# Turning finished attention results in three batches per head pair instead of tile by tile, in a two-layer streaming encoder on one Trainium2 core

## What is computed

```python
# layer 0: latent attention of 8 heads, then the shared output projection
s = (q_lat . ckv + q_rope . krope) * MLA_SCALE
p = softmax(where(visible, s, -inf));  o_lat = p @ ckv
x = x + concat([ha, hb], -1) @ w_out          # hb: o_lat through w_uv
# layer 1: band attention, 16 heads, a frame sees its chunk and the 8 before it
s = (q . k) * C_SCALE + rel_bias[:, idx]
p = softmax(where(valid, s, -inf));    o = p @ v
x = x + o.reshape(..., C_WIDTH) @ w_out_c
```

## Time and profile before

| | |
|---|---|
| median of 3 runs | 3217.87 us |
| lowest, highest | 3217.01, 3220.33 us |
| the profiled execution's own time | 3225.16 us |
| its span, first to last instruction | 3223.4 us |
| mean granted TensorE clock | 0.978 of 2.4 GHz |
| mix0b, its attention loop | about 504 to 799 us |
| mix1, its attention loop | about 1702 to 2364 us |

### The profile page before, as it was taken

How to read it: one execution, slowest core, us unless ns; L and a number is a source line. 1 busy time by engine, 2 the same in 40 slices (tenths; PEclk the granted TensorE clock), 3 DMA queues, 4 the chain that set the end, 5 groups by cost and what they waited for, 6 DMA issues and landing times. The chain is left out here.

```text
span 3223.4 us, 46994 instructions
## 1 busy us (share of the span) xinstructions
PE 3048.7 (95%) x18992; PEld 2941.0 (91%) x18992; DVE 1134.7 (35%) x2568; ACT 976.0 (30%) x1665; POOL 853.0 (26%) x436
## 2 busy tenths in 40 slices
PE   6999997999899999999989999999989999999998
PEld 5889896888799999999979999999869999999997
DVE  4423245566322222222243444444552222222223
ACT  4322234443412121111134444444442111211211
POOL 3212112110423222222242323223233222232320
PEclk8999998999899999999999999999989999999999
DMA  3133143110211211111021111111121111111101
GB/s 116 57 74 60 54 159 98 52 50 14 79 40 39 65 39 52 39 39 39 0 80 38 44 44 41 44 38 36 34 66 53 39 39 39 39 53 52 42 11 62
DMA packets 153854, 165.75 MB, mean 51 GB/s; under 512 B 9062, under 2 KB 137014, under 8 KB 153534
## 3 DMA queue, kind: packets, MB, share of 16 engines
q1 hardware_dynamic: 153726, 163.96, 16.7%
HBM read 140.78 MB, written 28.92 MB: 53 GB/s over the span
## 5 line engine op out<-in xcount | busy, mean ns | idle before, releaser
L236 PE MATMUL ffn_banks<-hhi,ffn_whi 128*128 128x384 f32 (+1 forms) x2112 | 692.2, 328 | 19.4 <-POOL hlo L217 13.6
L238 PE MATMUL ffn_banks<-hhi,ffn_wlo 128*128 128x384 f32 (+1 forms) x2112 | 691.7, 327 | 0.0
L237 PE MATMUL ffn_banks<-hlo,ffn_whi 128*128 128x384 f32 (+1 forms) x2112 | 691.6, 327 | 0.0
L236 PEld LDWEIGHTS ffn_banks<-hhi,ffn_whi 128*128 128x128 f32 x2112 | 399.4, 189 | 20.9 <-issue 20.9
L1118 POOL TENSOR_TENSOR ffn_wlo<-ffn_stage,ffn_whi 128x2048 fp32r<-128x2048 f32 x66 | 303.4, 4609 | 419.1 <-ACT ffn_whi L1078 419.1
L1184 DVE TENSOR_TENSOR ffn_act<-ffn_silu,ffn_banks 128x384 f32<-128x384 f32 x132 | 70.0, 532 | 962.6 <-PE ffn_banks L238 946.2
L237 PEld LDWEIGHTS ffn_banks<-hlo,ffn_whi 128*128 128x128 f32 x2112 | 399.3, 189 | 0.0
L238 PEld LDWEIGHTS ffn_banks<-hhi,ffn_wlo 128*128 128x128 f32 x2112 | 399.1, 189 | 0.0
L1190 DVE TENSOR_TENSOR xT<-xT,ffn_banks 128x384 f32<-128x384 f32 (+1 forms) x528 | 280.8, 532 | 240.6 <-PE ffn_banks L238 240.6
L238 PE MATMUL ffn_banks<-ffn_ahi,ffn_wlo 128*128 128x384 f32 (+1 forms) x1056 | 344.2, 326 | 0.0
L237 PE MATMUL ffn_banks<-ffn_alo,ffn_whi 128*128 128x384 f32 (+1 forms) x1056 | 344.1, 326 | 0.0
(11 more groups left out here) (329 smaller groups left out, 5436.8 us busy)
## 6 DMA issues: line engine op xcount, KB each, us to landing
ffn_stage<-in_w_gate SPq DMA_DIRECT2D x22, 1024.0 KB
ffn_stage<-in_w_up SPq DMA_DIRECT2D x22, 1024.0 KB, 5.4
ffn_stage<-in_w_down SPq DMA_DIRECT2D x22, 1024.0 KB, 4.8
mix_wst<-in_w_qkv SPq DMA_DIRECT2D x24, 512.0 KB
mix_wst<-in_w_in SPq DMA_DIRECT2D x22, 512.0 KB
load_xin<-in_x_prompt SPq DMA_DIRECT2D x8, 512.0 KB, 4.4
mix0b_wst<-in_w_out SPq DMA_DIRECT2D x8, 512.0 KB
mix_wst<-in_w_out SPq DMA_DIRECT2D x8, 512.0 KB
```

What stands on the lines that cost most here:

```text
L236: nc.tensor.matmul(out, whi[:, k, :], hhi[:, k, c0:c0 + w], start=(k == 0), stop=False)
L237: nc.tensor.matmul(out, whi[:, k, :], hlo[:, k, c0:c0 + w], start=False, stop=False)
L238: last = nc.tensor.matmul(out, wlo[:, k, :], hhi[:, k, c0:c0 + w], start=False, stop=(k == kts - 1))
```

## The change

Finished tiles of a head pair are transposed in three batches. In mix0b: tile 8, then 4 to 7, then 0 to 3. In mix1: tiles 0 to 3, then 8, then 4 to 7. A batch of four writes its four transposes side by side into one bank (512 columns) and signals once; ScalarE copies it with one instruction and VectorE subtracts with one. A batch comes where the flip of its last tile came: steps 10 and 14 of a pair and step 0 of the next in mix0b, steps 13 and 14 and step 0 of the next in mix1. The number of transposes stays at 108; copies and subtractions go from 108 to 36 each.

Two waits move with it. In mix0b the last output projection (`behind`) takes the chunks from the last to the first, and its first chunk waits for batch 1 alone, not for the one just turned. In mix1 every output projection waits for batch 0 ahead of chunk 0 and for batch 2 ahead of the others. In mix1 the planner of banks sees fewer entries, so the banks of other fillers shift.

```diff
@@ -1577,14 +1577,18 @@
-    behind = groups[(UNITS - 1) * PER:]
+    behind = [(UNITS - 1, j, c) for c in reversed(range(NC)) for j in range(KT)]
     FB = 3
+    TURNS = [(SAMPLE,), (4, 5, 6, 7), (0, 1, 2, 3)]
+
+    def turn_step(b):
+        return N + max(ORDER[1].index(t) for t in TURNS[b])
...
         pair, n = divmod(g - 1, STEPS)
-        return [("flip", pair, ORDER[1][n - N])] if n >= N else []
+        return [("flip", pair, b) for b in range(len(TURNS)) if turn_step(b) == n]
@@ -1642,9 +1646,12 @@
-        def out_of(pair, t):
-            cols = slice(t * P, t * P + tile_width(t))
-            return [x[:, CAT0 + pair, cols] for x in (hhi, hlo)]
+        def width_of_turn(b):
+            return sum(tile_width(t) for t in TURNS[b])
+
+        def out_of(pair, b):
+            c0 = TURNS[b][0] * P
+            return [x[:, CAT0 + pair, c0:c0 + width_of_turn(b)] for x in (hhi, hlo)]
@@ -1725,21 +1732,23 @@
                 if x[0] == "flip":
-                    _, pair, t = x
-                    w = tile_width(t)
-                    pe.wait_ge(s["evicted"], STEPS * pair + N + ORDER[1].index(t) + 1)
+                    _, pair, b = x
+                    pe.wait_ge(s["evicted"], STEPS * pair + turn_step(b) + 1)
                     if n >= FB:
                         pe.wait_ge(emptied[n % FB], n // FB)
-                    nc.tensor.transpose(F[:, n % FB, 0:w], otok[0:w, t, :], S["ident"][0:w, 0:w]).then_inc(filled[n % FB], 1)
+                    for i, t in enumerate(TURNS[b]):
+                        w = tile_width(t)
+                        last = nc.tensor.transpose(F[:, n % FB, i * P:i * P + w], otok[0:w, t, :], S["ident"][0:w, 0:w])
+                    last.then_inc(filled[n % FB], 1)
                     return
...
                 c0, w = CHUNKS[c]
-                if (j, c) == (0, 0):
+                if j == 0:
                     pe.wait_ge(s["w_lo"], u + 1)
...
                     else:
-                        await_emptied(pe, ("flip", u - CAT0, ORDER[1][-1]))
+                        await_emptied(pe, ("flip", u - CAT0, 1 if c == NC - 1 else 2))
                 if n >= FB:
@@ -1860,9 +1869,9 @@
             def high(x):
-                _, pair, t = x
+                _, pair, b = x
                 await_filled(act, x)
-                nc.scalar.activation(out_of(pair, t)[0], F[:, number[x] % FB, 0:tile_width(t)], ACT.Copy).then_inc(s["hi"], 1)
+                nc.scalar.activation(out_of(pair, b)[0], F[:, number[x] % FB, 0:width_of_turn(b)], ACT.Copy).then_inc(s["hi"], 1)
@@ -1903,10 +1912,10 @@
                 if x[0] == "flip":
-                    _, pair, t = x
-                    hi, lo = out_of(pair, t)
+                    _, pair, b = x
+                    hi, lo = out_of(pair, b)
                     dve.wait_ge(s["hi"], flip_no[x] + 1)
-                    v.tensor_tensor(lo, F[:, n % FB, 0:tile_width(t)], hi, ALU.subtract).then_inc(emptied[n % FB], 1)
+                    v.tensor_tensor(lo, F[:, n % FB, 0:width_of_turn(b)], hi, ALU.subtract).then_inc(emptied[n % FB], 1)
                     return
@@ -1999,6 +2008,7 @@
     N = len(TILES)
+    TURNS = [(0, 1, 2, 3), (NT - 1,), (4, 5, 6, 7)]
     STEPS = 2 * N
@@ -2041,13 +2051,19 @@
+    def turn_step(b):
+        return N + max(TILES.index(t) for t in TURNS[b])
+
+    def cols_of_turn(b):
+        c0 = TURNS[b][0] * P
+        return slice(c0, c0 + sum(tile_width(t) for t in TURNS[b]))
+
     def fillers(p, s):
...
         x = []
-        if s > N:
-            x.append(("flip", p, TILES[s - N - 1]))
+        x += [("flip", p, b) for b in range(len(TURNS)) if turn_step(b) == s - 1]
         if s == 0 and p:
-            x.append(("flip", p - 1, TILES[-1]))
+            x.append(("flip", p - 1, len(TURNS) - 1))
         if s == 0:
@@ -2066,7 +2082,7 @@
     ahead += [("kc", 0, 0), ("vtok", 0, 0)]
-    behind = [("flip", PAIRS - 1, TILES[-1])] + [("out", PAIRS - 1, j, c) for j, c in outs]
+    behind = [("flip", PAIRS - 1, len(TURNS) - 1)] + [("out", PAIRS - 1, j, c) for j, c in outs]
@@ -2255,19 +2271,20 @@
                     c0, w = CHUNKS[c]
-                    if (j, c) == outs[0]:
+                    if j == 0:
                         pe.wait_ge(s["w_lo"], u + 1)
-                        await_emptied(pe, ("flip", pair, TILES[-1]))
+                        await_emptied(pe, ("flip", pair, len(TURNS) - 1 if c else 0))
                     wh, wl = (y[:, u % 2, j * P:(j + 1) * P] for y in (whi, wlo))
...
                 elif kind == "flip":
-                    _, pair, t = x
-                    w = tile_width(t)
-                    pe.wait_ge(s["evicted"], STEPS * pair + N + TILES.index(t) + 1)
-                    last = nc.tensor.transpose(dst[:, 0:w], otok[0:w, t, :], S["ident"][0:w, 0:w])
+                    _, pair, b = x
+                    pe.wait_ge(s["evicted"], STEPS * pair + turn_step(b) + 1)
+                    for i, t in enumerate(TURNS[b]):
+                        w = tile_width(t)
+                        last = nc.tensor.transpose(dst[:, i * P:i * P + w], otok[0:w, t, :], S["ident"][0:w, 0:w])
                 elif kind == "vtok":
@@ -2384,10 +2401,11 @@
                 elif x[0] == "flip":
-                    _, pair, t = x
-                    w = tile_width(t)
+                    _, pair, b = x
+                    cols = cols_of_turn(b)
                     await_filled(act, x)
-                    nc.scalar.activation(o_hi[:, pair % 2, t * P:t * P + w], bank(x)[:, 0:w], ACT.Copy).then_inc(s["hi"], 1)
+                    nc.scalar.activation(o_hi[:, pair % 2, cols], bank(x)[:, 0:cols.stop - cols.start], ACT.Copy)\
+                        .then_inc(s["hi"], 1)
                 elif x[0] == "ktok":
@@ -2467,11 +2485,11 @@
                 if kind == "flip":
-                    _, pair, t = x
-                    cols = slice(t * P, t * P + tile_width(t))
-                    dve.wait_ge(s["hi"], N * pair + TILES.index(t) + 1)
-                    ins = nc.vector.tensor_tensor(o_lo[:, pair % 2, cols], src[:, 0:tile_width(t)], o_hi[:, pair % 2, cols],
-                                                  ALU.subtract)
+                    _, pair, b = x
+                    cols = cols_of_turn(b)
+                    dve.wait_ge(s["hi"], len(TURNS) * pair + b + 1)
+                    ins = nc.vector.tensor_tensor(o_lo[:, pair % 2, cols], src[:, 0:cols.stop - cols.start],
+                                                  o_hi[:, pair % 2, cols], ALU.subtract)
                 elif kind == "kc":
```

## The result

The changed kernel takes **3180.89 us** (median of 4 runs, 3177.63 to 3186.08) against 3217.44 us for the kernel before (4 runs, 3216.17 to 3220.33). The ratio is 0.9887, with a 95% interval of 0.987 to 0.9904: 36.6 us faster. The forecast was 3188, 30 us faster, and its range of 3180 to 3204 holds the time. The profiled execution took 3186.08 us, with a span of 3184.3, so it lies 5 us over its own median, and 39.1 us under the profiled execution of before.

The account below looks back on a forecast made before the run. TensorE, busy 95% of the span, was taken to lose time waiting for flips' banks and tiles. Gains of 20.5 us in mix1 and 10.1 in mix0b, about 30 off the 3217.9 median, gave 3188 us, range 3180 to 3204.

Parts of the forecast that it names:

- Which waits go, mix1: Mix1 steps 10, 11, 15, 16, 17 lose waits for flips: 4.13 us a pair, 24.8 us for six pairs.
- The batch's price of 0.40 us: Waits behind a batch of four grow by 0.40 us: 5.2 us in mix1 steps 13 and 0.
- Step 17: Mix1 step 17: the 0.77 us wait for the flip's bank falls to 0.12, gaining 0.65 us a pair.
- Mix0b: Waits in steps 11, 12, 16 and 17 go, less costs in steps 14, 18 and 0: 10.1 us gained.
- the lateness of 0.5 us behind the batch in step 0: Mix0b step 0: the batch delays VectorE's next maximum, making the next exponential 0.5 us late in three pairs, costing 1.5 us.
- the 0.2 us three times in step 18: Mix0b: turn(18) waits for its exponential once step 17's wait goes, giving 0.2 us back in three pairs.
- The tail of mix1: End of mix1: the 0.95 us wait goes, the third group waits about 0.4, transposes add 0.33; gain 0.2 us.
- Rival 1: Each batch costs its whole 0.73 us, as work isn't covered; gain 21 us, 3197, or 3207 with added lateness; chance 0.12.
- Rival 2: Mix1 steps 15 to 17: waits return as waits for VectorE's late adds; gain of 10 us, 3208; chance 0.04.
- Rival 3: Batches delay evict, the next maximum and the loop in narrow steps; at 2.0 us a batch, slower, 3227; chance 0.03.
- Rival 4: Another filler holds the same bank at the same step, so the time stays at 3218; chance 0.02.
- Rival 5: Batches fully covered and no lateness after step 0 in mix0b; 39 us gained, 3179 to 3183; chance 0.06.

Follow-up runs that it names:

- e8: Changed kernel with one more unread ScalarE copy of 192 columns ahead of each batch of four's copy; 3194.12 us, ratio 0.9922.
- e5: Changed kernel with mix1's load and split of the next v weights moved from step 16 to step 17; 3178.95 us, ratio 0.9887.
- e3: Kernel before, still one flip a tile, with each flip moved behind its step's other fillers; 3199.14 us, ratio 0.9941.
- second pair of profiles: Changed kernel and kernel before, both unedited, run and profiled once more on two other chips; 3183.12 us and 3220.50 us.
- e7: Changed kernel with batches of two tiles instead of four in both stages, still first among the fillers; 3185.12 us, ratio 0.9893.
- e9: Kernel before with single flips last among their step's fillers and mix1's v weight split in step 17; 3191.42 us, ratio 0.9916.
- e6: Changed kernel with batches last among their step's fillers and mix1's v weight split in step 17; 3174.59 us, ratio 0.9869.
- e11: Changed kernel with batches last among their step's fillers and mix1's v weight split moved earlier, to step 15; 3170.92 us, ratio 0.9849.

## Why the prediction was right, and where it was not

**Which waits go, mix1.** Right in mechanism; a pair was to get 3.3 us shorter and got 88.12 - 85.33 = 2.79. Steps 10, 11, 15 and 16 lost what they were to lose; what is left in 15 and 16 is 0.21 us each instead of 0.15. The batch's price of 0.40 us in steps 13 and 0 of mix1 was met to 0.01. e8 shows that this is a price of the queue: what ScalarE needs longer comes out at TensorE.

**Step 17, a mis-sized term.** "0.77 - 0.12 = 0.65 for step 17" gave 0.77 - 0.66 = 0.11. The step that failed is the question what is late next: it was asked of VectorE's adds alone, with the durations of the trace before. But VectorE also has `set_near` there, and reaching it earlier put it beside GpSimd's split, where it took 0.94 us instead of 0.34. That is 6 x 0.54 = 3.2 us. e5 takes the meeting away and a pair gets 0.58 us shorter; e3 makes it complete and it costs 2.26 us a pair. With it the pair's sum is 4.13 - 0.80 - 0.54 - 0.12 (0.06 more in each of 15 and 16) = 2.67 against 2.79 measured. Mix1 gave 17.7 us instead of 20.5, and 18.9 in the second pair of profiles.

**Mix0b, two mis-sized terms.** 12.7 and 11.4 us instead of 10.1. What failed first is the lateness of 0.5 us behind the batch in step 0, three times, and the 0.2 us three times in step 18: together 2.1 us were put down for them. Waits of turn for the exponential only grew from 5.5 to 5.7 us, the 0.2 being one wait at turn(18) of pair 0. The second goes the other way: the batch's price in step 14 was 0.52 to 0.59 us instead of 0.40, 2.2 instead of 1.6 in all; why it is higher than in mix1 isn't shown. With these measured the sum is 6.8 + 0.5 + 1.8 + 4.6 - 0.2 - 2.2 + 0.1 = 11.4. In the tail the third group waits 0.80 us, and the first no longer 0.90, as forecast: 0.1. The clock records may account for the rest in the first profiles: 13.7 us at the lower level before, 9.8 after, at most 2 us of time.

**A term that was missing.** The sum had nothing for stretches that the change doesn't touch. They were 8.7 and 11.5 us shorter in the profiles, of which 4 to 5 us, ahead of mix1, repeat with the kernel, and the medians fell by 36.6 us with 30.4 in the attentions. The size is measured, and for that one stretch the clock fits as its cause; why the clock changed isn't known.

**What was luck.** Within the attentions the sum came out at 30.6 us against 30.4. That is luck: mix1 had been put 2.8 us too high and mix0b 2.6 too low. The 7 us between 3188 and 3180.89 are of the missing kind, and the time lies only 0.9 us inside the range.

**The tail of mix1.** The 0.95 us of the earlier trace rows are gone and no group waits for the bank of batch 2. Less the 0.33 us of three more transposes that is 0.6 instead of 0.2; from the last flip to the first matmul of the norm it takes 17.12 us where it took 17.66.

**The rivals.** Rival 1, the full price: refuted, as steps 13 and 0 of mix1 cost 0.40 and step 14 of mix0b 0.52 to 0.59. Rival 2, adds that start late: they start 0.07 us after the reciprocal begins. Rival 3 decides from 1.6 us a batch, four times what a batch cost. Rival 4: the planner left step 15 free of the flip's bank. Rival 5 has the right time, 3179 to 3183, for a wrong reason: batches aren't fully covered. Of the signs of being wrong none came, but one was near: a matmul behind a batch waited up to 1.49 us, with 1.5 as the limit. The 0.66 us of step 17 are over 0.3, but stand behind a copy of V and not behind the adds.

**The rule against the change.** The waits behind a batch did get longer, 0.63 and 1.17 us for 0.24 and 0.77, so what the Trainium skill says in Perfetto Trace Analysis, "Optimizing Scalar/DVE Operations", that breaking instructions up may get work done sooner on engines that cause bubbles without being saturated, holds for one flip. It doesn't hold for the sum: e7 has half the size and pairs 0.82 us longer. What counted is how many times a pair TensorE asks for a bank that stands in two queues, and how much work is at hand while it does. Which of the two is worth more depends on the stage. In mix0b single flips last (294.3 us) beat batches first (298.0). In mix1 batches first (660.8) beat single flips last (677.0, and 671.6 in e9). Batches last have both, and their attentions are 12.1 us shorter than with batches first.

## What to carry to other kernels

A small piece of work that holds a shared buffer while it passes through two other engines' queues costs by where it stands and how often, more than by its size. Put it last among the work of its step and make it rare, and try each alone: which pays more depended on the stage here, and both together paid most. When a wait goes, everything behind it arrives earlier; list what it will now run beside, above all instructions from SBUF to SBUF on VectorE against long ones on GpSimd, and move the one whose time is free, here the split by one step; then look again, as a later split cost waits for its weights (e6, e9) and an earlier one met the same instruction in the first pair (e11). Compare unchanged stretches too, with their clock, before a whole difference is put down to the edit.

## What the runs showed of the hardware that was not expected

- An instruction of VectorE from SBUF to SBUF (`set_near`, 128x256) took 0.34 us alone, 0.94 us when the last 0.80 us of a 2.37 us split on GpSimd ran beside it, and 2.55 us when the whole split did: it ended when GpSimd ended, in both cases, plus 0.14 to 0.16 us. An add to `xT`, with one operand in PSUM, was not slowed: one of 128x320 that ran wholly beside a split took 0.49 us, six of the same shape behind it 0.48 to 0.49.
- Two copies on ScalarE one behind the other start 0.21 us apart though the first is recorded with 0.31 us.
- The mean granted clock of a program of 3200 us moved from 0.976 to 0.980 up to 0.980 to 0.982 with edits that leave the number of TensorE's instructions as it was. An unchanged stretch of 887 us got 4 to 5 us shorter with it.
- Waits of TensorE of 2.1 to 2.3 us, in e3 and e9, were followed within 1.3 us by a stretch at the lower clock level in seven of twelve cases, and pairs with such a stretch took 1.5 to 3.2 us longer.
